# A routed-experts stage: the experts' order made ahead of the early tokens, and the next norm's squares partly summed by DVE

## The chip, the core and the metric

The kernel runs on one core of a Trainium2 chip. The metric is the device time of one execution in microseconds (us). Engines: TensorE (PE: matmuls and transposes, with weight loads PEld that overlap them), VectorE (DVE), ScalarE (ACT), GpSimd (POOL) and SyncE (SP, which issues most DMAs).

## What is computed

Two blocks of a transformer are computed in one program for 512 tokens of 1024 channels, all in 32-bit floats. The first block (a gated delta mixer and a feed-forward) isn't touched. The second has two layers, "even" and "odd"; each is a norm, a mixer, a norm and a layer of experts. The experts are what matters here:

```python
h = _rms(x, norm2_w[layer]) * (1 + scale2) + shift2
x = x + gate2 * _hier_moe(h, ...)

def _hier_moe(h, w_group, b_group, w_expert, b_expert, w1, w3, w2):
    g_logits = xt @ w_group + b_group                 # 4 groups
    g_sel = argmax(g_logits)
    e_logits = (xt @ w_expert + b_expert)             # 8 experts in each group
    top_v, top_i = lax.top_k(e_in, 2)                 # two of the group's eight
    gate = p_g * softmax(top_v)
    # for each of 32 experts e, over its tokens xr:
    (silu(xr @ w1[e]) * (xr @ w3[e])) @ w2[e]         # 1024 -> 512 -> 1024
    # times the gate, summed into the token's row
```

Layer 1 ("odd") begins with a norm of the x that layer 0's experts leave: x / sqrt(mean(x*x) + eps), times a weight.

## The kernel before

x stands transposed in on-chip memory, as 8 pieces (k = 0 to 7) of 128 channels by 512 tokens. `experts(layer, ...)` is one block in which each engine runs a list of steps of its own; the engines meet only through semaphores, and each list is worked off in order. The block runs twice, from about 1690 to 2230 us (layer 0) and from about 2545 to the end (layer 1).

**Routing** (`route`). PE makes the logits (L2556 to L2565), transposes h to rows of tokens, which ACT stores in HBM for the gathers, and counts the tokens of each expert (L2571 to L2578). DVE makes from these, in a long list of small steps, first the selection matrices A of the two experts that are always computed first ("early", `FIXED` = 2), then the `order` of all experts by their count of tokens (L2669 to L2677), then for each token its slot (L2681 to L2737). `do(...)` is an instruction after which DVE waits for itself, since the next one reads its result. PE multiplies A with the rows (L2583) to have expert 0's tokens transposed, and makes the numbers of expert 1's tokens (L2589); DVE copies these (L2673) for POOL's gather of expert 1 (L2884). When DVE's list has come to L2737, PE makes the tokens of each slot (L2596), DVE copies them (L2739) for the other gathers, and PE spreads slots and weights over rows (L2601), which ACT copies out.

**Experts**. There are 15 units (`KINDS = "wwqpwpqwpwqwppq"`): "w" is one expert with a tile of 128 slots, "p" two experts with 64 each, "q" four with 32 each. Each expert has six loads of weights of 1 MB: four for `hidden` (w1 and w3, L2917), two for `output` (w2, L2941). SP issues all loads in order of use (L2823) into a ring of `MOE_RING` = 14 slots: load n waits until PE has used load n - 14. The first ten belong to experts 0 and 1, so they need no order. Ahead of load 10 SP waits for the order (L2841) and reads the numbers of the experts from it.

PE's list for unit i: the first half of `hidden(i)`, `turn(i + 1)` (transposes of the gathered tokens, L2900, which wait for the gather), `aturn(i - 1)` (L2927), the second half of `hidden(i)`, `output(i - 1)`, `scattered(i - 2)` (L2955: eight products that bring the rows back to the tokens, one for each k). In unit 0 the placing (L2596, L2601) stands after the second half of `hidden(0)`. After each of the scattered products DVE adds the result, times the gate, to x (`add`, L3081). Two banks are used for these in turn, so product n waits for add n - 2.

**Tail**. For the last unit the list is: output half 0, scattered k = 0 to 3, output half 1, scattered k = 4 to 7. DVE's list: adds 0 to 3, `out` (the copy of half 1's result, L3067), adds 4 to 7. In layer 0 ACT squares each piece of x when its add is through (`norm_squares`, L2806), and PE sums the squares over the channels with a matrix of ones, one product for each k (`norm_totals`, L2811): those of k = 0 to 3 ahead of output half 1, those of k = 4 to 7 after the last scattered product. ACT makes the norm's factor from the sum (L3049, L3050). A product of 32-bit floats appears as two records in the trace.

Of the kernel before, what the change touches and what calls it, by code (L numbers as in the profile page):

```python
# [17 lines left out]
ALU = mybir.AluOpType  # L18
# [5 lines left out]
KD = D // P  # L24
# [10 lines left out]
FIXED = 2  # L35
# [114 lines left out]
class Program:  # L150
# [1228 lines left out]
    squares = 0  # L1379
# [1113 lines left out]
    def route(self, layer):  # L2493
# [8 lines left out]
        def new(a, b):  # L2502
# [36 lines left out]
        s = {n: self.sem("route_" + n) for n in ["lg", "turned", "kept", "stored", "e", "ex", "oh", "rank", "ab", "tok",  # L2539
                                                 "order", "slots", "early", "early_made", "halves", "halves_kept", "early_tok",  # L2540
                                                 "place_made", "placed"]}
# [6 lines left out]
        toks, early_toks = small[:, 320:320 + BLOCKS], self.bank[4][:, 0:FIXED]  # L2548
# [72 lines left out]
        def vector_steps(dve):  # L2621
            def do(ins):
                self.dve.after(dve, ins)
# [45 lines left out]
            do(dve.tensor_tensor(kf, self.C("bonus"), cn, ALU.add))  # L2669
            do(dve.tensor_tensor(grid, across(key), rows32(key), ALU.is_gt))  # L2670
            do(dve.tensor_reduce(pf, grid, AX.X, ALU.add))
            dve.wait_ge(s["early_made"], 1)
            dve.tensor_copy(self.early_tok[:, 1:FIXED], early_toks[:, 1:FIXED]).then_inc(s["early_tok"], 1)  # L2673
            do(dve.tensor_tensor(grid, across(place), counted, ALU.is_equal))
            do(dve.tensor_tensor(grid, grid, c3("iota_e", 32), ALU.mult))  # L2675
            do(dve.tensor_reduce(picked.rearrange("p a b -> p (a b)"), grid, AX.X, ALU.add))  # L2676
            dve.tensor_copy(self.order, picked.rearrange("p a b -> p (a b)")).then_inc(s["order"], 1)  # L2677

            dve.wait_ge(s["ex"], 2)

# [62 lines left out]
    def experts(self, layer, job, gate):  # L2743
# [22 lines left out]
        N = len(seq)  # L2766
# [4 lines left out]
        for i in range(N - 1):  # L2771
            first13[i] = n
            n += 4 * len(seq[i][1])
            if i >= 1:
# [8 lines left out]
        s = {n: self.sem("moe_" + n) for n in ["turned", "kept0", "kept1", "used", "silu", "a", "aturned", "akept",  # L2783
                                               "yk0", "yk1", "spread", "scatter", "summed", "added"]}
# [8 lines left out]
        def spares(eng):  # L2793
            return eng.value_load(self.spare[0:1, OVF:OVF + 1], min_val=0, max_val=OVF) > 0
# [6 lines left out]
        spare_added = self.sem(f"moe_spare{layer}_added")  # L2801
        if layer == 0:
            sq, ss, squares = self.sem("odd1_squares"), self.sem("odd1_sums"), self.view(f, KD, L)

        def norm_squares(act, k):
            act.activation(squares[:, k, :], self.x[:, k, :], ACT.Square).then_inc(sq, 1)  # L2806

        def norm_totals(pe, ks):
            for k in ks:
                pe.wait_ge(sq, k + 1)  # L2810
                mm = pe.matmul(self.bank[0][:, :], self.C("ones"), squares[:, k, :], start=(k == 0), stop=(k == KD - 1))  # L2811
            if ks[-1] == KD - 1:
                mm.then_inc(ss, 1)

        with nc.Block() as block:
            @block.sync
# [74 lines left out]
            def _(pe):  # L2891
# [86 lines left out]
                aturn(N - 1)  # L2978
                output(N - 1, [0])
                scattered(N - 1, [0])  # L2980
                if layer == 0:
                    norm_totals(pe, range(4))
                output(N - 1, [1])
                scattered(N - 1, [1])
                if layer == 0:
                    norm_totals(pe, range(4, KD))
                with pe.If(any_spare):
                    pe.wait_ge(s["added"], KD * N)
                    spare_tensor(pe)
                    if layer == 0:  # L2990
                        pe.wait_ge(spare_added, KD * OVF)
                        pe.wait_ge(sq, 2 * KD)
                        norm_totals(pe, range(KD))

            @block.scalar
            def _(act):
# [55 lines left out]
            @block.vector  # L3052
            def _(dve):
                def keep(i):
                    dve.wait_ge(s["turned"], i + 1)
                    dve.tensor_copy(xT[i % 2][:, 4:8, :], self.bank[1][:, :].rearrange("p (a b) -> p a b", a=4)  # L3056
                                    ).then_inc(s["kept1"], 1)

                def akeep(i):
                    dve.wait_ge(s["aturned"], i + 1)  # L3060
                    dve.tensor_copy(aT, self.bank[6][:, :].rearrange("p (a b) -> p a b", a=4)).then_inc(s["akept"], 1)

                def out(i):
                    dve.wait_ge(s["used"], end2[i])
                    if i >= 2:
                        dve.wait_ge(s["summed"], KD * (i - 1))
                    dve.tensor_copy(y[i % 2][:, 512:1024], self.bank[6][:, :]).then_inc(s["yk0"], 1)  # L3067

                def spread(i):
                    if i == 0:  # L3070
                        dve.wait_ge(self.placed, 4)
                    if i >= 2:
                        dve.wait_ge(s["summed"], KD * (i - 1))
                    if i >= 1:
                        dve.wait_ge(s["scatter"], i)
                    self.spread(dve, scatter[i % 2], seq[i][0], s["spread"], i + 1).then_inc(s["scatter"], 1)

                def add(i, ks=range(KD)):
                    for k in ks:
                        dve.wait_ge(s["summed"], KD * i + k + 1)  # L3080
                        dve.scalar_tensor_tensor(self.x[:, k, :], self.bank[4 + k % 2][:, :], gate[:, k:k + 1],  # L3081
                                                 self.x[:, k, :], ALU.mult, ALU.add).then_inc(s["added"], 1)

                self.scale_steps(dve, [job], scaled)
                route_vector(dve)
                def gated(i):
                    dve.wait_ge(s["silu"], i + 1)
                    dve.tensor_tensor(a[i % 2], a[i % 2], self.bank[3][:, :], ALU.mult).then_inc(s["a"], 1)  # L3088

                for i in range(N - 1):  # L3090
                    if FIXED <= i + 1 < N:
                        keep(i + 1)
                    if i >= 1:
                        akeep(i - 1)
                    gated(i)
                    if i >= 1:
                        out(i - 1)
                    if i >= 2:
                        add(i - 2)
                    if i >= 1:  # L3100
                        spread(i - 1)
                akeep(N - 2)
                add(N - 3)
                spread(N - 2)
                out(N - 2)
                add(N - 2)
                spread(N - 1)
                any_spare = spares(dve)
                gated(N - 1)
                akeep(N - 1)  # L3110
                add(N - 1, [0, 1, 2, 3])
                out(N - 1)
                add(N - 1, [4, 5, 6, 7])
                if layer == 0:
                    self.gains(dve, self.S("norm1_2", 8, 16), self.mod["odd"][:, 8:16])
                with dve.If(any_spare):
                    dve.wait_ge(s["added"], KD * N)
                    spare_vector(dve)
# [291 lines left out]
```

## Time and profile before

| what | us |
|---|---|
| median of 3 runs (lowest, highest) | 3090.06 (3087.45, 3093.63) |
| profiled execution, its own time | 3087.26 |
| its span in the trace | 3085.5 |
| PE busy | 2816.3 (91%) |
| DVE busy | 1483.2 (48%) |
| ACT busy | 645.0 (21%) |
| DMA queue q1, share of the 16 engines | 48.1% |
| mean granted clock of PE | 0.953 |

The busy shares are means over stages of very different kinds, and a busy PE isn't PE at full speed: its clock is granted at one of two levels, and the column PEclk gives it as a share of the full one. The experts stages are to be read by themselves, with windows, timelines and what ended the idle time of an engine.

### The profile page before, as it was taken

The numbers are of one execution on the slowest core, as the hardware profiler recorded it, in microseconds if no ns is written. First come the engines' busy times: TensorE is split into PE (matmuls) and PEld (weight loads), VectorE is DVE, ScalarE is ACT, GpSimd is POOL, SyncE is SP. The second block draws the span as 40 slices with busy tenths as digits, with TensorE's granted clock in tenths as the row PEclk, the third lists the DMA queues.
The fourth block names the chain that finished last, engine by engine and source line by source line (L and its number), as shares of the span: only waits on it lengthen the run. The fifth ranks groups of instructions, "written<-read, shape, count | busy, mean of one in ns | idle before, by whom it ended". The sixth has DMA issues, their size and how long they took to land. (4 is left out here: it accounts for less than half of the span.)

```text
span 3085.5 us, 36648 instructions
## 1 busy us (share of the span) xinstructions
PE 2816.3 (91%) x14052; PEld 1813.9 (59%) x14052; DVE 1483.2 (48%) x2937; ACT 645.0 (21%) x1350; POOL 158.1 (5%) x169
## 2 busy tenths in 40 slices
PE   6989779999988998999889989999799899899997
PEld 4877657788946887877764533333278545333332
DVE  4576565566735677336543423324355724333334
ACT  3111454445621111010232100000202422000000
POOL 0000021212200000000010000000000000000000
PEclk8999989999999999999979999999999998999999
DMA  6111146663022232222103799999632036999997
GB/s 249 50 46 55 69 152 246 246 246 137 15 95 69 82 90 74 83 69 78 60 1 143 287 420 419 420 419 420 241 112 82 15 153 231 410 418 419 420 419 313
DMA packets 112920, 614.83 MB, mean 199 GB/s; under 512 B 12944, under 2 KB 13408, under 8 KB 62944
## 3 DMA queue, kind: packets, MB, share of 16 engines
q1 hardware_dynamic: 102464, 576.67, 48.1%
q0 software_dynamic: 9120, 31.49, 2.9%
q10 hardware_dynamic: 1152, 4.19, 0.3%
q8 instruction: 118, 1.93, 0.3%
q14 instruction: 66, 0.54, 0.1%
HBM read 603.79 MB, written 8.51 MB: 198 GB/s over the span
## 5 line engine op out<-in xcount | busy, mean ns | idle before, releaser
L2917 PE MATMUL bank<-arena 128*32 128x512 f32 (+2 forms) x2048 | 429.6, 602 | 15.8 <-DMA arena<-in_w 14.8
L440 PE MATMUL bank<-arena 128*128 128x256 f32 x1776 | 411.9, 387 | 33.2 <-DVE arena L493 10.8
L440 PEld LDWEIGHTS bank<-arena 128*128 128x128 f32 x1776 | 341.6, 193 | 99.6 <-issue 34.5
L2917 PEld LDWEIGHTS bank<-arena 128*32 128x32 f32 (+2 forms) x2048 | 148.6, 134 | 269.8 <-issue 268.9
L2941 PE MATMUL bank<-arena 128*32 128x512 f32 (+2 forms) x1024 | 230.8, 661 | 36.4 <-DMA arena<-in_w 36.4
L2955 PE MATMUL bank<-arena 128*128 128x512 f32 x480 | 235.4, 614 | 10.5 <-DVE arena L3129 4.9
L253 PE MATMUL bank<-arena 128*128 128x512 f32 (+1 forms) x608 | 217.4, 517 | 14.8 <-DVE arena L652 13.9
L3081 DVE SCALAR_TENSOR_TENSOR arena<-bank,arena 128x512 f32<-128x512 f32 x240 | 180.3, 751 | 81.3 <-PE bank L2955 68.5
L2941 PEld LDWEIGHTS bank<-arena 128*32 128x32 f32 (+2 forms) x1024 | 78.3, 143 | 184.9 <-issue 184.8
L253 PEld LDWEIGHTS bank<-arena 128*128 128x128 f32 x608 | 119.3, 197 | 110.2 <-issue 101.5
L2955 PEld LDWEIGHTS bank<-arena 128*128 128x128 f32 x480 | 76.6, 188 | 167.2 <-DVE arena L3081 96.5
L3088 DVE TENSOR_TENSOR arena<-arena,bank 128x512 f32<-128x512 f32 x30 | 20.7, 688 | 220.1 <-ACT arena L3023 220.1
L2999 ACT ACTIVATE arena<-bank 128x512 f32<-128x512 f32 x30 | 17.9, 597 | 504.7 <-PE bank L2900 480.2
L3067 DVE COPY arena<-bank 128x512 f32<-128x512 f32 x30 | 20.8, 692 | 205.2 <-PE bank L2941 205.2
L1475 PE MATMUL bank<-arena 128*128 128x256 f32 x528 | 118.0, 379 | 0.0
L1111 ACT ACTIVATE arena<-bank 128x256 f32<-128x256 f32 x288 | 93.6, 382 | 88.3 <-PE bank L1031 65.9
L1475 PEld LDWEIGHTS bank<-arena 128*128 128x128 f32 x528 | 100.0, 189 | 14.4
L1031 PE MATMUL bank<-arena 128*128 128x128 f32 x576 | 98.4, 293 | 1.7 <-DVE arena L1226 1.0
L1031 PEld LDWEIGHTS bank<-arena 128*128 128x128 f32 x576 | 75.3, 190 | 40.0 <-issue 31.6
L1223 DVE TENSOR_TENSOR arena<-bank,arena 128x256 f32<-128x256 f32 x144 | 61.0, 424 | 76.8 <-PE bank L1016 76.7
L1016 PE MATMUL bank<-arena 128*128 128x128 f32 x576 | 94.4, 287 | 0.6
L3056 DVE COPY arena<-bank 128x512 f32<-128x512 f32 x26 | 18.0, 692 | 148.9 <-PE bank L2900 148.9
(452 smaller groups left out, 4152.3 us busy)
## 6 DMA issues: line engine op xcount, KB each, us to landing
arena<-in_w SPq DMA_DIRECT2D x384, 1024.0 KB, 19.4
arena<-in_dense SPq DMA_DIRECT2D x308, 512.0 KB, 4.5
arena<-core_rows POOLq DMA_DIRECT2D x48, 256.0 KB, 6.6
arena<-in_xT SPq DMA_DIRECT2D x2, 2048.0 KB, 12.6
token_rows<-arena ACTq DMA_DIRECT2D x8, 512.0 KB, 2.6
gdn_gate<-arena POOLq DMA_DIRECT2D x8, 256.0 KB, 2.6
arena<-gdn_gate SPq DMA_DIRECT2D x1, 2048.0 KB, 8.3
arena<-band_bias POOLq DMA_DIRECT2D x2, 1024.0 KB, 6.0
```

What stands on the lines that cost most here:

```text
L253: mm = eng.matmul(dst, w[:, k, :], src[:, k, :], start=(k == 0), stop=(k == KD - 1))
L440: mm = pe.matmul(out, w[:, k, :], x[:, k, :], start=(k == 0), stop=(k == K1 - 1))
L1016: mm = pe.matmul(Y[u][:, q, :], buf[u]["bl"][:, q, :], buf[u]["xl"][:, u, q, :], start=True, stop=True)
L1031: mm = pe.matmul(touched(X[u][:, 2 * q:2 * q + 2, :], l, u), buf[u]["zs"][:, q, :], buf[u]["yn"][:, q, :], start=False, stop=(l == 6), ski ...
L1111: act.activation(gathered(buf[u]["xl"][:, side, :, :], l + 1), touched(X[u], l + 1, side), ACT.Copy).then_inc(kept, 1)
L1223: dve.tensor_tensor(buf[u]["yn"], Y[u][:, 0:2, :], levels[:, l - 1, :, :].to_broadcast([P, 2, P]), ALU.mult).then_inc(s["yn"], 1)
L1475: mm = pe.matmul(product(m, p), s4[:, t, k, :], ht[:, t, k, :], start=(k == 0), stop=(k == K1 - 1))
L2917: mm = pe.matmul(self.bank[2 + t][part, :], xT[i % 2][:, 2 * q + k, part], w[j][:, k, t, :], start=(q == 0 and k == 0), stop=(q == 3 and k ...
L2941: mm = pe.matmul(self.bank[7 - t][part, :], aT[:, k, part], w[j][:, k, :], start=(k == 0), stop=(k == 3))
L2955: pe.matmul(self.bank[4 + k % 2][:, :], y[i % 2][:, k * P:(k + 1) * P], scatter[i % 2], start=True, stop=True).then_inc(s["summed"], 1)
L3067: dve.tensor_copy(y[i % 2][:, 512:1024], self.bank[6][:, :]).then_inc(s["yk0"], 1)
L3081: dve.scalar_tensor_tensor(self.x[:, k, :], self.bank[4 + k % 2][:, :], gate[:, k:k + 1], self.x[:, k, :], ALU.mult, ALU.add).then_inc(s[" ...
```

## The change

In three places of `route` and `experts`:

1. `route`, DVE's list: the wait for PE's early tokens and their copy (L2673) move from ahead of L2674 to behind L2677. The order is then made ahead of the copy. This holds in both layers.
2. `experts`, tail of layer 0: PE no longer multiplies each of the eight pieces of squares with the ones. DVE adds the squares of k = 1 to 6 to those of k = 0 in place, three sums behind add 3 and ahead of `out`, one behind add 5, one behind add 6, one behind add 7. Each waits for ACT's square, and all but the last are followed by a wait of DVE for itself. PE multiplies the gathered sum and, apart from it, the squares of k = 7, with the ones (two products), both behind the last scattered product.
3. The rare case in which an expert has more tokens than its slots hold (`any_spare`) calls `norm_totals` over all eight as before.

The scattered products and the output halves keep their places.

```diff
@@ route, DVE
             do(dve.tensor_reduce(pf, grid, AX.X, ALU.add))
-            dve.wait_ge(s["early_made"], 1)
-            dve.tensor_copy(self.early_tok[:, 1:FIXED], early_toks[:, 1:FIXED]).then_inc(s["early_tok"], 1)
             do(dve.tensor_tensor(grid, across(place), counted, ALU.is_equal))
             do(dve.tensor_tensor(grid, grid, c3("iota_e", 32), ALU.mult))
             do(dve.tensor_reduce(picked.rearrange("p a b -> p (a b)"), grid, AX.X, ALU.add))
             dve.tensor_copy(self.order, picked.rearrange("p a b -> p (a b)")).then_inc(s["order"], 1)
+            dve.wait_ge(s["early_made"], 1)
+            dve.tensor_copy(self.early_tok[:, 1:FIXED], early_toks[:, 1:FIXED]).then_inc(s["early_tok"], 1)
@@ experts, PE
                 scattered(N - 1, [0])
-                if layer == 0:
-                    norm_totals(pe, range(4))
                 output(N - 1, [1])
                 scattered(N - 1, [1])
                 if layer == 0:
-                    norm_totals(pe, range(4, KD))
+                    pe.wait_ge(gathered_sums, 1)
+                    pe.matmul(self.bank[0][:, :], self.C("ones"), squares[:, 0, :], start=True, stop=False)
+                    pe.wait_ge(sq, KD)
+                    pe.matmul(self.bank[0][:, :], self.C("ones"), squares[:, KD - 1, :], start=False, stop=True).then_inc(ss, 1)
@@ experts, DVE
+                def sum_square(k):
+                    dve.wait_ge(sq, k + 1)
+                    return dve.tensor_tensor(squares[:, 0, :], squares[:, 0, :], squares[:, k, :], ALU.add)
+
                 add(N - 1, [0, 1, 2, 3])
+                if layer == 0:
+                    for k in range(1, 4):
+                        self.dve.after(dve, sum_square(k))
                 out(N - 1)
-                add(N - 1, [4, 5, 6, 7])
+                add(N - 1, [4, 5])
+                if layer == 0:
+                    self.dve.after(dve, sum_square(4))
+                add(N - 1, [6])
+                if layer == 0:
+                    self.dve.after(dve, sum_square(5))
+                add(N - 1, [7])
+                if layer == 0:
+                    sum_square(6).then_inc(gathered_sums, 1)
                 if layer == 0:
                     self.gains(dve, self.S("norm1_2", 8, 16), self.mod["odd"][:, 8:16])
```

## Rows read from the trace of the kernel before

**Rows 1.** The page, costliest groups: busy and mean ns, then idle time and its releaser.

```profile
L2941 PE MATMUL bank<-arena 128*32 128x512 f32 (+2 forms) x1024 | 230.8, 661 | 36.4 <-DMA arena<-in_w 36.4
```

**Rows 2.** Windows of 10 us: length, PE, PEld, DVE, ACT, POOL busy, PEclk, DMA share, GB/s.

```profile
1750.00:1760.00 10.00, 10.00 (x24) 4.35 (x23) 1.03 (x2) 0.78 (x2) 0.23 (x1) 1.00 0.89 310
1770.00:1780.00 10.00, 9.91 (x83) 3.94 (x80) 1.53 (x3) 1.20 (x2) 0.94 (x1) 1.00 1.01 423
...
2210.00:2220.00 10.00, 9.45 (x46) 3.05 (x44) 3.05 (x5) 2.52 (x4) 0.00 (x0) 1.00 0.01 4
```

**Rows 3.** Timeline of PE, layer 0: start, duration, engine, line, operation, count, idle before.

```profile
1721.54 1.04 PE L2900 MATMUL bank<-arena 128*128 128x128 f32 x8
1722.41 7.05 PE L2917 MATMUL bank<-arena 128*128 128x512 f32 x16
1732.81 3.59 PE L2596 MATMUL bank<-arena 128*128 128x31 f32 x16 [3.35 <-DVE arena L2737]
...
1741.10 7.05 PE L2917 MATMUL bank<-arena 128*128 128x512 f32 x16
```

**Rows 4.** Timeline of DVE, POOL and SP's queue in the routing of layer 0.

```profile
1714.25 0.16 DVE L2673 CAST arena<-bank 128x1 uint32<-128x1 f32 x1 [7.06 <-PE bank L2589]
...
1715.25 1.19 POOL L2884 DMA_INDIRECT arena<-token_rows,arena  x1 [115.26 <-DVE arena L2673]
...
1718.09 0.18 DVE L2677 CAST arena<-arena 128x32 int32<-128x32 f32 x1
1718.18 0.16 DVE L2681 TENSOR_REDUCE arena<-arena 128x4 f32<-128x16 f32 x1
...
1720.91 42.81 SPq L2823 DMA_DIRECT2D arena<-in_w  x14
```

**Rows 5.** Short windows, columns as in rows 2: PE's clock around two gaps.

```profile
1732.00:1733.00 1.00, 0.19 (x1) 0.22 (x2) 0.63 (x3) 0.00 (x0) 0.00 (x0) 0.50 0.98 410
1738.00:1739.00 1.00, 1.00 (x8) 1.00 (x7) 0.00 (x0) 0.60 (x1) 0.82 (x1) 0.60 1.02 426
...
1914.00:1917.00 3.00, 0.51 (x6) 0.21 (x4) 0.69 (x1) 0.60 (x1) 0.00 (x0) 1.00 1.01 421
```

**Rows 6.** POOL's gathers: all 28, then the one issued at 1749.29 (DMA view).

```profile
DMA to landing us min/median/max: 4.5/8.6/9.9
...
arena<-token_rows,arena POOLq DMA_INDIRECT x1, 5.9
```

**Rows 7.** Timeline of layer 1: POOL's gather of expert 1 and PE.

```profile
2572.28 1.25 POOL L2884 DMA_INDIRECT arena<-token_rows,arena  x1 [285.90 <-DVE arena L2673]
2578.62 1.04 PE L2900 MATMUL bank<-arena 128*128 128x128 f32 x8
...
2589.90 3.59 PE L2596 MATMUL bank<-arena 128*128 128x31 f32 x16 [3.36 <-DVE arena L2737]
...
2599.66 7.05 PE L2917 MATMUL bank<-arena 128*128 128x512 f32 x16
```

**Rows 8.** Timeline of the tail of layer 0.

```profile
2181.36 0.69 DVE L3129 TENSOR_TENSOR arena<-arena 128x512 f32<-128x512 f32 x1
...
2211.61 1.61 DVE L3081 SCALAR_TENSOR_TENSOR arena<-bank,arena 128x512 f32<-128x512 f32 x2 [0.36 <-PE bank L2955]
...
2212.26 3.60 PE L2811 MATMUL bank<-arena 128*128 128x512 f32 x8
...
2215.80 3.65 PE L2941 MATMUL bank<-arena 128*32 128x512 f32 x32
...
2219.59 0.69 DVE L3067 COPY arena<-bank 128x512 f32<-128x512 f32 x1 [6.37 <-PE bank L2941]
...
2221.50 1.61 DVE L3081 SCALAR_TENSOR_TENSOR arena<-bank,arena 128x512 f32<-128x512 f32 x2 [1.22 <-PE bank L2955]
...
2224.13 3.61 PE L2811 MATMUL bank<-arena 128*128 128x512 f32 x8
...
2225.12 0.63 ACT L2806 ACTIVATE arena<-arena 128x512 f32<-128x512 f32 x1 [0.23 <-DVE arena L3081]
```

More of the change, by code:

```diff
@@ L2803, in experts, with norm_totals @@
             sq, ss, squares = self.sem("odd1_squares"), self.sem("odd1_sums"), self.view(f, KD, L)
+            gathered_sums = self.sem("odd1_gathered_sums")
         def norm_squares(act, k):
             act.activation(squares[:, k, :], self.x[:, k, :], ACT.Square).then_inc(sq, 1)
-        def norm_totals(pe, ks):
-            for k in ks:
-                pe.wait_ge(sq, k + 1)
+        def norm_totals(pe):
+            for k in range(KD):
                 mm = pe.matmul(self.bank[0][:, :], self.C("ones"), squares[:, k, :], start=(k == 0), stop=(k == KD - 1))
-            if ks[-1] == KD - 1:
-                mm.then_inc(ss, 1)
+            mm.then_inc(ss, 1)
         with nc.Block() as block:
@@ L2992, in _ @@
                         pe.wait_ge(sq, 2 * KD)
-                        norm_totals(pe, range(KD))
+                        norm_totals(pe)
             @block.scalar
```

## The prediction

> **What bounds the kernel now.** I read the page first: one core, a span of 3085.5 us, and the largest waits of TensorE (PE) inside the experts stages are on weight loads, 36.4 us of idle time ahead of L2941 over both layers [rows 1]. Next come windows of 10 us over the experts stage of layer 0, for the DMA column. From 1770 us on the queues move 423 GB/s and the 16 engines are full; that goes on for some 390 us with PE waiting now and then. Between 1750 and 1760, however, they move only 310 GB/s [rows 2]. There the ring of 14 slots is full: SP can issue a load only when PE has used a slot, and in the first two experts, which keep whole tiles of tokens ("w"), PE needs about 3.5 us a slot. So near the start of the stage **PE sets the time of the loads**, and from the first block with four experts ("q") on, the loads set the time of PE. Whatever PE gains ahead of about 1763 us moves the whole stream of loads, and with it the end of the stage; what only the loads gain ahead of that point is lost against the full ring. The same holds in layer 1.
>
> So I then read PE's timeline ahead of that point. PE runs the first half of expert 0, turns the tokens of expert 1 (1721.54), runs the second half (1722.41 to about 1729.46), stands idle for 3.35 us on DVE's L2737, does the placing of the slots (L2596, L2601) from 1732.81, and starts expert 1 at 1741.10 [rows 3]. The idle time is the end of DVE's long chain of routing steps. That chain itself was held up before: DVE waited 7.06 us for PE's early tokens (L2673) and only then made the order [rows 4]. The third view is PE's clock in windows of 1 us: in the gap it fell to half (0.50, that is 1.2 of 2.4 GHz) by 1732 and came back only within 1738 to 1739 [rows 5].
>
> **The order of the experts ahead of the tokens (both layers).** The four instructions L2674 to L2677 move into DVE's wait of 7.06 us. The order, ready at 1718.27 now, is then ready about 7.1 us earlier, at 1711.2. The copy of the early tokens waits for PE as before and stays at 1714.25, so the gather that POOL issues at 1715.25 isn't issued later. What stands behind the copy (L2681 on) starts at 1714.4 in place of 1718.18, 3.8 us earlier [rows 4], and the chain's end, now 1732.8, comes at 1729.0: just ahead of PE, which is through with expert 0 at 1729.46 [rows 3]. The idle time of 3.35 us closes; next late is PE itself.
>
> SP issued its first load that depends on the order 2.6 us after the order, at 1720.91 [rows 4]. It will do so at about 1713.8. Four slots are free, and the next ones wait for PE as before. The earlier loads gain nothing by themselves: the load after the first eight has to wait for the first quarter of expert 1 (now 1741.10 + 3.5 = 1744.6), and eight loads of 1 MB at 420 GB/s are through 20 us after their start, before it in either kernel.
>
> But they take something. Today the gather of expert 1's tokens (0.5 MB, issued at 1715.25) runs on idle DMA engines: it lands after 4.5 us, the minimum of all 28 gathers [rows 6], at 1719.75, and PE wants it at 1721.54 [rows 3]. In the changed kernel 4 MB of weights are ahead of it in the engines, 10 us of work. Beside a full queue 24 of the 28 gathers landed after 8.0 to 9.9 us, median 8.6; beside a queue with one load or so it was 5.9 [rows 6]. Here the queue is full, so I take 8.6: landing at 1723.85, and **PE waits 2.3 us at the turn of expert 1**, which delays its second half and all behind it. Bounds: 0 (5.9 and below) and 3.6 us (9.9). Layer 1 has the same: issue 2572.28, wanted at 2578.62, so 8.6 gives 2.3 us [rows 7].
>
> The trace shows both kinds of DMA, SP's loads and POOL's gather, slowing each other down [rows 6]. The Trainium skill, "DMA: Bandwidth & Descriptors", section "Issuing engines are not separate DMA queues", says the same in general: copies issued by different engines end up on the same 16 DMA engines and interleave. Its section "Queues, rings and completion order" adds that an engine takes turns between the queues, which would leave the gather a half share and speaks for the rival "gather in time" below; the trace's 8.6 beside 4.5 speaks against it.
>
> **The clock while slots are placed.** L2596 and L2601 are 48 records of small matmuls. At half clock they took 8.29 us in layer 0 (1732.81 to 1741.10) [rows 3], partly, as the clock came back in their midst, and 9.76 us in layer 1 [rows 7]. At full clock eight records of the kind take 0.87 us (1721.54 to 1722.41) [rows 3], 0.109 each, so 48 take 5.2 us. Without the gap the clock has no reason to fall there: I book 3.1 us for layer 0 and 4.5 us for layer 1. Bounds: nothing, if it falls all the same, and these values.
>
> The new wait of 2.3 us is a gap of its own. In the 3 us from 1914, of which PE worked 0.51, a gap of 2.49, the clock stayed at 1.00 [rows 5], and the gap in which it fell was 3.35 us [rows 3]. I take it that it stays, but not by much. If it falls there, it is at half for 6.8 us as from 1732 to 1738.7 [rows 5], and costs 3.4 us in that layer.
>
> Layer 0: 3.35 - 2.3 + 3.1 = 4.1 us gained; layer 1: 3.36 - 2.3 + 4.5 = 5.6 us [rows 3, 7].
>
> **The sums of squares by DVE (layer 0 only).** Two groups of eight records (four products each) with the ones matrix, 3.54 and 3.61 us, leave PE [rows 8]. The first stood ahead of the last output half (2212.26, output at 2215.80), on the chain, and its 3.54 us are gained: the queues move 4 GB/s from 2210 on [rows 2], so the weights have landed, and DVE isn't late for the copy L3067 (2219.59, then 2216.05): its adds 0 to 3 end at 2213.22, and three sums at some 0.73 us (0.69 of L3129 and its own wait) end at 2215.4 [rows 8]. They are covered by 0.6 us; without it they would cost their own length less that. L391 and L392 come later by the same time as the last sum and are wanted by nobody before the norm is made. The scatters stay where they stand, so none is added or moved.
>
> The second group is replaced by three more sums on DVE's chain and two products (four records). Taken from the first late add (2221.50 now): adds 4 and 5 end at +1.61, sum 4 at +2.34, add 6 at +3.13, sum 5 at +3.85, add 7 at +4.63, sum 6 at +5.35; ACT's last square, begun at the end of add 7 (+3.62 now), ends at +5.29. PE starts at +5.45 and needs 4 x 0.43 and the last drain, 1.9 us: +7.35. Now its eight records run from 2224.13 (+2.63) to +6.24 [rows 8]. So 1.1 us is given back: net 2.4 us. PE is idle for about 2.9 us ahead of them, and if the clock falls there, four records take 1.7 us more; net 0.7 us. The next stage starts when all engines are out of this one, so the gain is carried on.
>
> **Sum.** 4.1 + 5.6 + 2.4 = 12.1 us. The profiled execution took 3087.26 us (span 3085.5), 2.8 below the median of the runs; I subtract from the median: 3090.06 - 12.1 = 3078.0 us.
>
> **The rivals.**
> "Clock falls at the new wait": for it speaks that 2.3 us is near gaps at which it fell, against it the gap of 2.49 us. One layer: 12.1 - 3.4 = 8.7, 3081.4 us; both: 5.3, 3084.8 us.
> "Gather in time": it lands in under 6.3 us as if the queue were nearly empty, because each engine serves it in turn. PE doesn't wait: 12.1 + 4.6 = 16.7, 3073.4 us. For it speaks the 5.9 us gather; against it 24 of 28.
> "The placing stays at half clock", because the tiny matmuls don't keep it: 1.0 + 1.1 + 2.4 = 4.5 us, 3085.6 us. Against it: the clock in the rows fell in the idle stretch, not in the matmuls.
> "Gather behind the backlog" (the other side): the engines work off SP's six loads first, 6 MB or 15 us from 1714.9 (1.1 after the first issue, an estimate), then the gather, which lands at about 1732; PE waits 10.6 us a layer and its clock falls: layer 0 is 3.35 - 10.6 + 3.1 - 3.4 = 7.5 us worse, layer 1 6.2, less 2.4 of the tail: 11.3 us slower, 3101.4 us. It decides the sign from the point at which the wait passes 5 us (12.1 - 6.8 = 2 x 2.65 beyond the 2.3 booked), a landing of some 11.3 us, which none of the 28 had.
> That the order doesn't come earlier at all can't be: nothing else holds the four instructions.
>
> **How the numbers follow.** Forecast 0.40; the clock falls at the wait in one layer 0.25, in both 0.09; gather in time 0.10; placing at half clock 0.10; gather behind the backlog 0.06. The runs before spread by 6 us, and a measurement can tell about 0.2%, 6 us. Faster by more: forecast, one layer and gather in time, 0.75, less 0.07 because 8.7 us is near the border: 0.68. Within: 0.26, slower 0.06. The range goes from just under the gather in time to just over the placing at half clock, 3071.5 to 3087, which leaves out the backlog and the edges.
>
> **What would show it.** Right: L2677 ahead of L2673 at about 7 us before where it stood; SP's first load near 1713.8; an idle time of some 2.3 us of PE ahead of the L2900 of expert 1 with the gather as its releaser; none ahead of L2596; clock 1.00 through L2596 and L2601, and about 5.2 us for both; L2941's last half right behind the scatters; four records of the ones matrix that start about 5.4 us after add 4. Wrong: a gather that lands in 5 us, clock 0.50 at the turn of expert 1 or in the placing, or an end of the stage that doesn't move with the start of expert 1.

## The result and the profile after

The changed kernel takes 3081.96 us (median of 8 runs, 3077.2 to 3084.16), the kernel before, run on the same chips, 3092.64 us (8 runs, 3087.45 to 3098.32). The ratio is 0.9964 [0.9953, 0.9975]: **11.1 us faster**, 7.7 to 14.5. The forecast was 3078.0 us (3071.5 to 3087.0), a gain of 12.1 us. Time, range and sign held. The reasons held less well than the total, as the traces show. The profiled execution took 3077.2 us, 10.1 less than the one of before.

The page of the changed kernel: the span, and the group that answers to [rows 1] (L2940 is before's L2941, `output`).

```profile
span 3074.4 us, 36633 instructions
...
L2940 PE MATMUL bank<-arena 128*32 128x512 f32 (+2 forms) x1024 | 232.2, 664 | 36.4 <-DMA arena<-in_w 36.4
```

PE's waits on the weights of `output` are the same 36.4 us; with those of `hidden` the page has 49.0 us in all, where before it was 51.2. They hardly shrink, although experts start earlier: the stream of loads from HBM still bounds the middle of the stage. What changed stands at its two ends.

**Start of the stage, layer 0.** Timeline of the changed kernel, to be held against [rows 3, 4]: start, duration, engine, line, operation, count, idle time before it and its releaser. L2916 is `hidden`, L2899 `turn`, L2883 the gather, L2822 SP's loads; L2675 now makes the order, L2677 copies the early tokens.

```profile
1706.83 0.18 DVE L2675 CAST arena<-arena 128x32 int32<-128x32 f32 x1
1709.60 0.16 DVE L2677 CAST arena<-bank 128x1 uint32<-128x1 f32 x1 [2.60 <-PE bank L2589]
1709.64 47.71 SPq L2822 DMA_DIRECT2D arena<-in_w  x14
1710.00 7.12 PE L2916 MATMUL bank<-arena 128*128 128x512 f32 x16 [0.43 <-issue]
1710.61 1.03 POOL L2883 DMA_INDIRECT arena<-token_rows,arena  x1 [114.14 <-DVE arena L2677]
1719.88 1.76 PE L2899 MATMUL bank<-arena 128*128 128x128 f32 x8 [2.76 <-DMA arena<-token_rows,arena]
1721.44 8.10 PE L2916 MATMUL bank<-arena 128*128 128x512 f32 x16
1729.37 1.86 PE L2596 MATMUL bank<-arena 128*128 128x31 f32 x16
1731.08 3.82 PE L2601 MATMUL bank<-arena 128*128 128x128 f32 x32
1734.73 7.05 PE L2916 MATMUL bank<-arena 128*128 128x512 f32 x16
```

Read it from above. The order is there 2.8 us ahead of the early tokens' copy, where it used to come 4 us behind, and DVE's wait for PE has shrunk from 7.06 to 2.60 us. SP starts its loads 0.4 us before PE starts expert 0; before, 6.3 us after. POOL's gather is issued 1 us behind them, among them. PE then stands idle 2.76 us at the turn of expert 1, with the gather as releaser: a wait that the kernel before doesn't have. There is no gap ahead of the placing (L2596) any more, and the placing takes 5.36 us (1729.37 to 1734.73) in place of 8.29.

How long the first transfers took (DMA view of the changed kernel; the last number is us from issue to landing):

```profile
arena<-in_w SPq DMA_DIRECT2D x2, 1024.0 KB, 8.8
arena<-token_rows,arena POOLq DMA_INDIRECT x1, 9.2
```

The gather of 0.5 MB, which took 4.5 us on idle DMA engines, takes 9.2, in both layers.

PE's clock in windows of 1 us, columns as in [rows 2], the clock behind POOL's share:

```profile
1719.00:1720.00 1.00, 0.12 (x1) 0.12 (x2) 0.86 (x6) 0.00 (x0) 0.00 (x0) 1.00 0.97 406
1720.00:1721.00 1.00, 1.00 (x6) 1.00 (x7) 0.90 (x4) 0.00 (x0) 0.00 (x0) 0.57 1.03 434
1722.00:1723.00 1.00, 1.00 (x2) 0.34 (x1) 0.97 (x2) 0.98 (x3) 0.00 (x0) 0.50 0.97 410
1723.00:1724.00 1.00, 1.00 (x3) 0.53 (x2) 0.96 (x3) 1.00 (x1) 0.00 (x0) 0.72 1.03 434
1730.00:1731.00 1.00, 1.00 (x12) 1.00 (x11) 0.00 (x0) 0.17 (x1) 0.00 (x0) 1.00 0.99 246
```

The clock fell behind the new wait, from about 1720.1, and was back within 1723 to 1724; in the placing it stands at 1.00. From the start of the turn to that of the placing it is 9.49 us (1719.88 to 1729.37); where the same work ran at full clock, in e3_loads_after_gather below, it is 7.75 (1724.68 to 1732.43). The dip costs 1.7 us.

Layer 1 shows the same (timeline of the changed kernel, against [rows 7]):

```profile
2563.11 7.12 PE L2916 MATMUL bank<-arena 128*128 128x512 f32 x16 [0.43 <-issue]
2572.95 1.51 PE L2899 MATMUL bank<-arena 128*128 128x128 f32 x8 [2.72 <-DMA arena<-token_rows,arena]
2574.26 8.36 PE L2916 MATMUL bank<-arena 128*128 128x512 f32 x16
2582.45 1.86 PE L2596 MATMUL bank<-arena 128*128 128x31 f32 x16
2587.81 7.05 PE L2916 MATMUL bank<-arena 128*128 128x512 f32 x16
```

**Tail of layer 0.** Timeline of the changed kernel, against [rows 8]: L3113 are DVE's sums, L2984 and L2986 the two products with the ones, L3049 ACT's factor of the norm.

```profile
2201.39 1.61 DVE L3081 SCALAR_TENSOR_TENSOR arena<-bank,arena 128x512 f32<-128x512 f32 x2 [12.73 <-PE bank L2954]
2204.11 3.65 PE L2940 MATMUL bank<-arena 128*32 128x512 f32 x32
2204.88 2.14 DVE L3113 TENSOR_TENSOR arena<-arena 128x512 f32<-128x512 f32 x3
2207.96 0.69 DVE L3067 COPY arena<-bank 128x512 f32<-128x512 f32 x1 [0.94 <-PE bank L2940]
2209.87 1.61 DVE L3081 SCALAR_TENSOR_TENSOR arena<-bank,arena 128x512 f32<-128x512 f32 x2 [1.22 <-PE bank L2954]
2214.16 0.68 DVE L3113 TENSOR_TENSOR arena<-arena 128x512 f32<-128x512 f32 x1
2214.90 1.94 PE L2984 MATMUL bank<-arena 128*128 128x512 f32 x2 [2.24 <-DVE arena L3113]
2216.63 1.91 PE L2986 MATMUL bank<-arena 128*128 128x512 f32 x2
2218.58 0.69 ACT L3049 ACTIVATE arena<-bank,arena 128x512 f32<-128x512 f32 x1 [2.37 <-PE bank L2986]
```

Two rows of the kernel before that are needed beside [rows 8], its add 0 and its factor:

```profile
2209.64 1.61 DVE L3081 SCALAR_TENSOR_TENSOR arena<-bank,arena 128x512 f32<-128x512 f32 x2 [12.84 <-PE bank L2955]
...
2227.77 0.69 ACT L3049 ACTIVATE arena<-bank,arena 128x512 f32<-128x512 f32 x1 [0.72 <-PE bank L2811]
```

The three early sums are hidden: DVE still waits 0.94 us for PE before it copies (L3067). From add 0 (2201.39) to add 4 (2209.87) it is 8.48 us; before it was 11.86 (2209.64 to 2221.50). That is the booked gain, 3.4 for 3.54. From add 4 to the factor, however, it is 8.71 us (2209.87 to 2218.58), where before it was 6.27 (2221.50 to 2227.77): 2.4 us given back in place of 1.1. PE was idle for 2.24 us ahead of L2984, and the clock was half behind it (window of the changed kernel):

```profile
2215.00:2216.00 1.00, 1.00 (x2) 0.49 (x3) 0.13 (x1) 1.00 (x1) 0.00 (x0) 0.54 0.00 0
```

**What the pair of traces adds up to.** From expert 0's start to expert 1's start: 26.52 and 28.00 us before (layer 0, layer 1), 24.73 and 24.70 after, so 1.8 and 3.3 us gained. The tail, from add 0 to the first step behind the norm, went from 19.93 to 18.84 us: 1.1. Together 6.2 us, while the spans differ by 11.1. Of that, 4.6 us lie ahead of expert 0, which begins at 1714.58 in the one trace and at 1710.00 in the other. DVE, too, reaches the moved place some 4 us earlier (at 1703.05, three instructions of 3.7 us ahead of 1706.83, against 1707.2, where its wait of 7.06 us began), so all but some 0.4 us of the difference is older than the first edited instruction. In the other traces of this study expert 0 begins anywhere from 1711.0 to 1717.7, whatever the edit; with one part of the change alone it begins at 1715.87 (e1) and 1713.79 (e2), so neither part brings the early start with it. Two spans alone would have made the gain look larger than what the edits did at their places.

### The profile page after: what moved, and what is told of

It is laid out like the page before. It is cut to its first block and busy times, and to the rows that moved or that the text cites. A ratio compares the mean times of both kernels' runs of the same rounds, so it can differ in the third digit from the quotient of the medians.

```text
span 3074.4 us, 36633 instructions
## 1 busy us (share of the span) xinstructions
PE 2808.3 (91%) x14040; PEld 1806.5 (59%) x14040; DVE 1486.5 (48%) x2943; ACT 645.5 (21%) x1350; POOL 158.0 (5%) x169
## 5 line engine op out<-in xcount | busy, mean ns | idle before, releaser
L2916 PE MATMUL bank<-arena 128*32 128x512 f32 (+2 forms) x2048 | 430.3, 600 | 13.5 <-DMA arena<-in_w 12.6
L440 PE MATMUL bank<-arena 128*128 128x256 f32 x1776 | 410.9, 386 | 33.4 <-DVE arena L493 10.9
L440 PEld LDWEIGHTS bank<-arena 128*128 128x128 f32 x1776 | 340.6, 193 | 100.9 <-issue 34.6
L2916 PEld LDWEIGHTS bank<-arena 128*32 128x32 f32 (+2 forms) x2048 | 149.5, 134 | 267.5 <-issue 266.5
L2940 PE MATMUL bank<-arena 128*32 128x512 f32 (+2 forms) x1024 | 232.2, 664 | 36.4 <-DMA arena<-in_w 36.4
L2940 PEld LDWEIGHTS bank<-arena 128*32 128x32 f32 (+2 forms) x1024 | 78.9, 143 | 185.6 <-issue 185.0
L3088 DVE TENSOR_TENSOR arena<-arena,bank 128x512 f32<-128x512 f32 x30 | 20.7, 688 | 216.2 <-ACT arena L3023 216.2
L3067 DVE COPY arena<-bank 128x512 f32<-128x512 f32 x30 | 20.8, 692 | 201.8 <-PE bank L2940 201.8
```

Source lines behind the costliest of these rows:

```text
L440: mm = pe.matmul(out, w[:, k, :], x[:, k, :], start=(k == 0), stop=(k == K1 - 1))
L2916: mm = pe.matmul(self.bank[2 + t][part, :], xT[i % 2][:, 2 * q + k, part], w[j][:, k, t, :], start=(q == 0 and k == 0), stop=(q == 3 and k ...
L2940: mm = pe.matmul(self.bank[7 - t][part, :], aT[:, k, part], w[j][:, k, :], start=(k == 0), stop=(k == 3))
```

## The experiments

All ran beside the kernel before. "Start" is the time from expert 0's start to expert 1's, "stream" the time from expert 0's start to that of the last unit's first output half (the last work that waits for weights), each for layer 0 / layer 1, in us.

| kernel | time, us (runs) | against before, us (interval) | start | stream |
|---|---|---|---|---|
| before | 3092.64 (8) | | 26.5 / 28.0 | 487.1 / 489.5 |
| after | 3081.96 (8) | -11.1 (-14.5 to -7.7) | 24.7 / 24.7 | 483.6 / 487.4 |
| e1_order_only | 3085.67 (11) | -5.9 (-9.0 to -2.8) | 24.9 / 25.0 | 487.4 / 486.3 |
| e2_squares_only | 3089.65 (11) | -1.2 (-4.0 to +1.5) | 27.9 / 28.0 | 489.5 / 489.7 |
| e3_loads_after_gather | 3075.36 (5) | -17.0 (-21.6 to -12.7) | 20.1 / 20.1 | 484.4 / 483.8 |
| e4_sum_early | 3078.42 (5) | -12.4 (-16.4 to -8.0) | 24.9 / 24.8 | 487.9 / 489.5 |
| e5_hold_and_tail | 3074.44 (4) | -16.4 (-20.7 to -12.1) | 20.1 / 20.1 | 483.6 / 484.0 |
| e6_loads_later | 3096.11 (1) | one run | 20.1 / 20.1 | 493.9 / 494.1 |
| e7_best | 3073.49 (6) | -16.7 (-21.0 to -12.4) | 20.1 / 20.1 | 483.3 / 483.5 |
| e8_pe_kept_busy | 3081.57 (1) | one run | 24.7 / 24.8 | 487.3 / 487.5 |

### Each part alone

`e1_order_only` is the kernel before with the order's move alone:

```diff
-            dve.wait_ge(s["early_made"], 1)
-            dve.tensor_copy(self.early_tok[:, 1:FIXED], ...).then_inc(s["early_tok"], 1)
             do(dve.tensor_tensor(grid, across(place), counted, ALU.is_equal))
...
             dve.tensor_copy(self.order, ...).then_inc(s["order"], 1)
+            dve.wait_ge(s["early_made"], 1)
+            dve.tensor_copy(self.early_tok[:, 1:FIXED], ...).then_inc(s["early_tok"], 1)
```

> The kernel before with the first part alone: order ahead of the early tokens, squares as before. My theory (the gain comes from PE's closed gap ahead of the placing and the clock kept there, less PE's new wait for the gather): from expert 0's first record to expert 1's about 24.7 us in both layers, as in the changed kernel, against 26.5 and 28.0 before; so 1.8 + 3.3 us in the two places, 5 us or, with what the stream of loads makes of it, up to 9 us faster than before. Rival (the part is worth nothing since loads that start earlier run into a wait anyway): within 2 us of before, and all of the gain in the other run, the squares.

`e2_squares_only` is the changed kernel with this move undone, so that only the tail of layer 0 differs from before:

> The kernel before with the second part alone: DVE sums the squares, order as before. My theory: 3.5 us gained at the output half, 1.1 us given back at the end with PE at full clock, 2.8 at half clock: 0.7 to 2.4 us faster than before, with the last ones products starting 5.0 to 5.5 us after add 4. Rival (the end of the stage is set by DVE's chain and the whole gain is given back): 0 or slower. The changed kernel was 11 us faster, of which its trace shows 4.6 us as arisen ahead of the first edited instruction: if the placement of code and not chance made those, one of the two single parts shows them too.

Measured: the order alone gives 5.9 us, the squares alone 1.2 us that can't be told from nothing. In e1 the wait at the turn is 2.95 and 3.02 us, the gather lands after 9.4 us, and the placing takes 5.36 us: all three belong to the order's move. In e2 add 4 to the factor takes 8.24 us, and the tail 18.37 us against 19.93: 1.6 us by its trace. What follows: the order carries the change. The two parts add up to 7.1 us, less than the 11.1 of both together, but the intervals overlap.

### The new wait belongs to the loads ahead of the gather

`e3_loads_after_gather` keeps the early order, but SP waits until the gather of expert 1 has landed before it issues loads that depend on the order:

```diff
                         sp.wait_ge(self.order_ready, 1)
+                        sp.wait_ge(x_in[1], x_in_before[1] + nth(1))
```

> The changed kernel, with SP waiting for the landing of expert 1's gather ahead of its first load that depends on the order. My theory (PE's wait of 2.8 us at the turn of expert 1 is the gather slowed by loads that nobody needs so early, and the ring has room): the gather lands after some 4.5 us in place of 9.2, PE's wait at L2899 goes, its clock stays full, expert 0 to expert 1 takes 20.5 us in place of 24.7, and the time falls by 2 x 4.3 = 8 to 9 us against the changed kernel, 20 us against before. Rival (the loads are needed early: the stream starts 6 us later and PE waits for weights instead): no gain or a loss against the changed kernel, with more DMA waits on the first q unit near 1765.

Measured: 3075.36 us, 17.0 less than before and 6.6 less than the changed kernel's median. The gather lands after 4.3 us. PE doesn't wait at the turn, which takes 1.03 us without idle time before it, and the start falls to 20.07 us in both layers. SP's first load now goes out 7.6 us after expert 0's start, later than in the kernel before (6.3), and it costs two waits on weights, 1.3 and 0.4 us, in the stretch from 1700 to 1800. So the wait of 2.8 us and the dip of the clock behind it come from the order's effect on the loads, and nothing of the order's gain comes from loads that start early.

`e6_loads_later` holds the loads still longer, until PE has used four slots:

```diff
                         sp.wait_ge(x_in[1], x_in_before[1] + nth(1))
+                        sp.wait_ge(s["used"], 4)
```

> The kernel with SP held until the gather landed, and held further until PE has used four slots, which is 14.8 us after expert 0's start: first load at about 17.5 us in place of 7.6. My theory (the loads have slack of a few us only: four free slots and four that PE frees early, 20 us of work, have to be through when PE frees the next at 23.6 us, and in the six frees after it the stream catches up 6 us): expert 0 to expert 1 stays 20.1 us, but PE's first waits for weights come in the first q unit near 42 to 60 us after expert 0's start, together 6 to 10 us in each layer, and the time is 10 to 20 us above the run with SP held. Rival (the start of the stream doesn't matter since the ring is full anyway): the same time as with SP held.

Measured (one run): 3096.11 us, some 21 more than e3, where 10 to 20 were expected. Experts 0 and 1 run as in e3. The first load comes 17.6 us after expert 0's start, and then the stream is late (e6_loads_later: SP's queue, PE, and its waits from 1700 to 1800):

```profile
1729.83 30.11 SPq L2822 DMA_DIRECT2D arena<-in_w  x18
...
1767.87 6.45 PE L2918 MATMUL bank<-arena 128*32 128x512 f32 x32 [4.97 <-DMA arena<-in_w]
...
1778.94 6.04 PE L2918 MATMUL bank<-arena 128*32 128x512 f32 x32 [4.63 <-DMA arena<-in_w]
...
PE bank L2918 <- DMA arena<-in_w: 9.6, 2, 5.0
```

Two waits of 5 us appear in the first block of four experts, and the stream ends 10 us a layer later than in e3. The prediction's picture of the stage is shown by this pair: loads that begin 7.6 us after expert 0's start cost PE next to nothing, loads that begin at 17.6 us set the time of the whole stream.

### The tail

In `e4_sum_early` DVE adds only k = 1 to 3. PE multiplies their sum ahead of the last scattered products, and then k = 4 to 7 one by one as in the kernel before:

```diff
@@ PE
                 output(N - 1, [1])
-                scattered(N - 1, [1])
                 if layer == 0:
                     pe.wait_ge(gathered_sums, 1)
                     pe.matmul(self.bank[0][:, :], self.C("ones"), squares[:, 0, :], start=True, stop=False)
-                    pe.wait_ge(sq, KD)
-                    pe.matmul(self.bank[0][:, :], self.C("ones"), squares[:, KD - 1, :], start=False, stop=True).then_inc(ss, 1)
+                scattered(N - 1, [1])
+                if layer == 0:
+                    for k in range(4, KD):
+                        pe.wait_ge(sq, k + 1)
+                        mm = pe.matmul(self.bank[0][:, :], self.C("ones"), squares[:, k, :], start=False, stop=(k == KD - 1))
+                    mm.then_inc(ss, 1)
@@ DVE
                 out(N - 1)
-                add(N - 1, [4, 5])
...
+                add(N - 1, [4, 5, 6, 7])
```

> The changed kernel with another tail: DVE sums the squares of k = 0 to 3 only, PE multiplies that sum in its gap ahead of the last scattered products, and multiplies k = 4 to 7 one by one behind them, as before. My theory (the second group's sums on DVE cost 2.4 us at the end: DVE's chain is longer and PE's clock falls while it waits): from add 4 to the norm's factor 6.3 us in place of 8.7, so 2 to 3 us faster than the changed kernel. Rival (the end is bound by ACT's squares, or the product in the gap holds up the scattered ones): no difference within 1 us, scattered products starting 0.9 us later.

Measured: 3078.42 us, 12.4 less than before. Its tail (e4_sum_early, timeline; L3084 is add 4):

```profile
2215.28 1.12 PE L2983 MATMUL bank<-arena 128*128 128x512 f32 x2
...
2217.41 1.61 DVE L3084 SCALAR_TENSOR_TENSOR arena<-bank,arena 128x512 f32<-128x512 f32 x2 [1.22 <-PE bank L2954]
...
2220.04 3.60 PE L2988 MATMUL bank<-arena 128*128 128x512 f32 x8
2223.68 0.69 ACT L3052 ACTIVATE arena<-bank,arena 128x512 f32<-128x512 f32 x1 [0.72 <-PE bank L2988]
```

Add 4 to the factor takes 6.27 us again, and the whole tail 16.73 us in place of 18.84 (after) and 19.93 (before). So by the traces the sum of the early squares is worth 3.2 us, and adding the late ones on DVE gave 2.1 of them back. Between the times of e4 and of the changed kernel (12.4 and 11.1 us gained) such a step can't be made out; where it went is shown under "Both together".

`e8_pe_kept_busy` asks why the late ones cost so much. It is the changed kernel with two products of squares with the ones that nobody uses, put into PE's gap:

```diff
                 if layer == 0:
+                    pe.wait_ge(sq, 4)
+                    for k in (1, 2):
+                        pe.matmul(self.bank[1][:, :], self.C("ones"), squares[:, k, :], start=(k == 1), stop=(k == 2))
                     pe.wait_ge(gathered_sums, 1)
```

> The changed kernel with two more products (four records, results unused) on PE behind the last scattered product, ahead of its wait for the gathered sum. My theory (the four records of the sum took 3.7 us since PE's clock fell in its gap of 2.2 us; DVE's chain is the other part of what was given back): with PE busy through the gap the clock stays 1.00, the four records take 1.9 us, and from add 4 to the norm's factor it is 7.0 us in place of 8.7. Rival (the records are slow for another reason, or the clock falls all the same): 8.7 us as before.

Measured (one run; e8_pe_kept_busy, timeline and a window of its tail; L2985 are the added products, L2987 and L2989 those of the sums):

```profile
2215.41 1.61 DVE L3084 SCALAR_TENSOR_TENSOR arena<-bank,arena 128x512 f32<-128x512 f32 x2 [1.22 <-PE bank L2954]
...
2218.04 1.88 PE L2985 MATMUL bank<-arena 128*128 128x512 f32 x4
...
2220.45 1.12 PE L2987 MATMUL bank<-arena 128*128 128x512 f32 x2 [0.53 <-DVE arena L3116]
2221.41 1.02 PE L2989 MATMUL bank<-arena 128*128 128x512 f32 x2
2222.47 0.69 ACT L3052 ACTIVATE arena<-bank,arena 128x512 f32<-128x512 f32 x1 [0.71 <-PE bank L2989]
...
2221.00:2222.00 1.00, 1.00 (x4) 0.36 (x2) 0.00 (x0) 0.76 (x1) 0.00 (x0) 1.00 0.09 25
```

With PE's gap down to 0.53 us the clock stands at 1.00, and add 4 to the factor takes 7.06 us. Against the 8.71 of the changed kernel that is 1.65 us: the clock. The other 0.8 us (7.06 against 6.27) is DVE's chain of sums itself. Work that nobody uses made the step shorter, which excludes that DVE's chain alone was the cause.

### Both together

`e5_hold_and_tail` is e3 with the tail of e4. `e7_best` has the same tail, with the hold put at the first load that depends on the order, in `load(n)`:

```diff
+                    if n == first13[FIXED]:
+                        sp.wait_ge(x_in[1], x_in_before[1] + nth(1))
                     if n >= MOE_RING:
```

> The same with SP held ahead of its reading of the experts' numbers, as in the run with SP held. My theory: its gain (17 us) and the tail's (2 to 3 us) add up: 19 us faster than before. Rival (they don't add, since what the tail gives goes into a wait for the next stage's weights): 17 us.

> The order ahead of the tokens, the gather of expert 1 protected, and the tail in which DVE sums only the squares of k = 0 to 3. SP waits for the gather at its first load that depends on the order, behind its reading of the experts' numbers (in the run before it waited ahead of the reading). My theory (in the run with SP held, PE's way from expert 0 to expert 1 was 20.1 us, 7.9 less than before, of which 4.9 a layer were left at the stage's end; the tail gave 3.2 us): 20.1 us again, SP's first load some 5 us after expert 0's start in place of 7.6, and 2 x 5 + 3 = 13 to 19 us faster than before, about 3073 us. Rival (the loads ahead of PE's need it were late by the holding, and a hold 2.6 us shorter gives back what was lost): 5 us or more faster than the run with SP held and the late sums.

Measured: 3074.44 and 3073.49 us, 16.4 and 16.7 less than before. Start of layer 0 in e7_best, a timeline and then the gather in the DMA view (L2901 is `turn`, L2824 SP's loads):

```profile
1711.03 7.12 PE L2918 MATMUL bank<-arena 128*128 128x512 f32 x16 [0.43 <-issue]
1716.10 3.09 SPq L2824 DMA_DIRECT2D arena<-in_w  x6
1717.99 1.03 PE L2901 MATMUL bank<-arena 128*128 128x128 f32 x8
...
arena<-token_rows,arena POOLq DMA_INDIRECT x1, 4.3
```

The first load goes out 2.5 us earlier than in e3 (5.07 against 7.56 us after expert 0's start) with no gain that can be seen: the slack of the loads once more. Nor does the tail of e4 show on top of the hold: 16.4 and 16.7 against 17.0, each within some 4 us, while the tails in the traces promise some 2. The traces show where it went, and it isn't a wait for the next stage's weights: from the tail's end (the first step behind the norm) to the next stage's first product (L440) it is 7.4 to 7.6 us with either tail. It went into PE's clock behind that. Of L440's records, the second group in the changed kernel and in e5 (timelines):

```profile
2236.55 1.97 PE L440 MATMUL bank<-arena 128*128 128x256 f32 x8 [2.91 <-DVE arena L493]
...
2237.11 2.84 PE L440 MATMUL bank<-arena 128*128 128x256 f32 x8 [3.64 <-DVE arena L493]
```

In all three kernels with the tail of e4 the first group ran at full clock from its start (5.13 us in e5, where it is 5.86 in the changed kernel), PE's gap behind it is 3.64 us in place of 2.91, and behind the gap the clock fell to half, which it didn't in the changed kernel. From L440's first record to the first one of a later step, L1801, it is 22.7 us in e4, e5 and e7, and 21.1 in the changed kernel, e3 and e6; and on to layer 1's expert 0 it is 337.3 to 337.5 against 335.3 to 335.4. That takes back the 2 us. Whether it must isn't shown, since kernels with one and the same tail differ there too: before and e1 (334.8 and 337.5), the changed kernel and e2 (335.3 and 336.5).

e3, e5 and e7 can't be told apart. All three beat the changed kernel's median, by 6.6 to 8.5 us. Their intervals against before overlap with that of the changed kernel, but only two of their 15 runs took longer than its fastest of eight, and in the traces expert 1 starts 4.6 us sooner after expert 0 in both layers.

## Why the prediction was right, and where it wasn't

**What bounds the kernel: right, but not all of a gain is carried.** The first two experts are PE's, the rest the loads': e3, e6 and e7 show both ends of it. The prediction then passed every microsecond gained at expert 1's start on to the end of the stage. Over all traces the start was 27.6 us (before and e2), 24.8 (after, e1, e4) and 20.1 (held: e3, e5, e7), and the stream's end 489.0, 487.1 (with e8's) and 483.8. Of 2.8 us gained 1.9 arrive, and of 7.5 us 5.2: **about two thirds**. The second pair is the firm one (the six held streams lie within 483.3 to 484.4, the four of before and e2 within 487.1 to 489.7); the single streams of the first scatter from 483.6 to 489.5, more than the 1.9 us themselves. A part of the loss are longer waits for weights, 51.2 us on the page of before, 53.9 in e3 and 52.1 in e7. Another shows at the wait about 327 us behind expert 0's start of layer 0: in the changed kernel PE goes on at 326.2, in before at 328.4, in e7 at 321.6. Behind it the same 32 products took 5.13 us in before and 6.61 in e7, as the clock was half behind the wait for more or less of them. That is up to 1.5 us; the rest isn't settled.

**DVE's order: right.** Ahead of the early tokens by 2.8 us, SP's first load 0.4 us before expert 0's start (forecast: 0.8 before), the gather issued no later (0.6 us behind expert 0's start, where it was 0.7), the gap of 3.35 us ahead of the placing gone in both layers. In both layers the placing came behind expert 0 without a wait.

**The gather: right in kind and nearly in size.** 9.2 us to land for 8.6, a wait of 2.76 and 2.72 for 2.3. The median of the gathers beside a full queue was the right row to take; "gather in time" and "gather behind the backlog" fell. The wait cost 0.4 us a layer more than booked. That SP's loads and the gather slow *each other* down is not in [rows 6], which shows the gather's side alone.

**The placing's clock: right.** 5.36 us for 5.2, at 1.00. "The placing stays at half clock" fell: the small matmuls keep the clock if PE comes to them without a gap.

**The clock at the new wait: the step that failed.** "I take it that it stays" rested on the one gap of 2.49 us in [rows 5]. It fell in both layers, which was the rival with 0.09, and in all six further waits of this kind (e1, e4, e8). Its price, though, was half of what the rival said: half speed for about 3.4 us, not the 6.8 of [rows 5], so 1.7 us a layer, not 3.4. With this, the sum at expert 1's start is, for layer 0, 3.35 - 2.76 + 2.93 - 1.74 = 1.8 us (measured 1.8, booked 4.1), and for layer 1 3.36 - 2.72 + 4.40 - 1.75 = 3.3 us (measured 3.3, booked 5.6). The terms close, so no other effect is missing there.

One gap at full clock was no ground for the step, and the traces show it with a gap that has the same length and the same work ahead of it in every kernel. PE multiplies 16 records of a unit's scatter, four records of `aturn`, waits 2.45 us for DVE and goes on with the next scatter. In layer 1 of before, then of the changed kernel (timelines):

```profile
3015.84 7.96 PE L2955 MATMUL bank<-arena 128*128 128x512 f32 x16 [2.45 <-DVE arena L3129]
...
3004.00 9.35 PE L2954 MATMUL bank<-arena 128*128 128x512 f32 x16 [2.46 <-DVE arena L3144]
```

The first runs at full clock, the second has half of it for 3.4 us and takes 1.4 us more. Over the ten traces and two layers this wait left the clock alone 8 times (7.96 us) and lowered it 12 times (9.35 to 9.57 us).

**The tail: the gain right, what was given back too small.** The early group's 3.54 us came off as booked and the three sums were hidden, with 0.94 us to spare for the 0.6 forecast. In the late part PE waited 2.24 us for the 2.9 forecast, the clock fell, and 2.4 us in place of 1.1 were given back. The prediction had named this end (net 0.7) and not taken it; measured is 1.1 in the pair of traces, 1.6 in e2. Both misses are one: a short gap of PE was taken to leave the clock alone, three times, and three times it didn't. In the tail the clock fell in all four kernels that have the gap of 2.24 us (the changed kernel, e2, e3, e6).

**The total: right in part because two errors met.** By the prediction's own steps, mended with the traces, the change is worth 6.2 us at its places, and less if only two thirds of the starts are carried (3.4 + 1.1 = 4.5 us). The two parts run alone add up to 7.1 us. The interval of the changed kernel, 7.7 to 14.5, lies above the traces' sums of 6.2 and 4.5. Part of the distance may be the kernel before, whose median was 3092.64 us in the eight runs beside the changed kernel, 3091.47 in the 21 beside e1 to e4 and 3089.77 in the 11 beside e5 and e7; against 3091.47 the changed kernel would be 9.5 us faster, against 3089.77 7.8. By these medians 2 to 5 us stay without a cause that a trace shows, and this is left open. The forecast of 12.1 overestimated the edits by some 6 us, and the remainder filled most of that: that the total came within 1 us of the forecast is luck.

## What to carry to other kernels

Before a load is made to start earlier, look at what is small, urgent and issued beside it: here 4 MB of weights that had 7 us of slack and more doubled the time of a 0.5 MB gather that had under 2 us (it landed at 1719.75 and was wanted at 1721.54), and one wait of the issuing queue for that gather gave about 6 us more than the change itself. A gap of 2 to 3 us in TensorE's work is to be booked with a dip of the clock behind it (some 1.7 us here), even where a trace shows that very gap at full clock: the next trace may not. And if a stage is bound by its loads, pass on only a part of what its first experts gain.

## What the runs showed of the hardware

- PE's clock fell to half behind gaps of 2.72, 2.76 and 2.24 us, though it had stood at 1.00 through one of 2.49 us [rows 5] and, in the changed kernel, through one of 3.52 us (ahead of 1807.00). Neither the length of the gap nor the work ahead of it decides: one and the same gap of 2.45 us lowered the clock 12 times of 20. What does decide, no run varied.
- How long it stays half differs too: 6.8 us behind a gap of 3.35 us [rows 5], about 3.4 us behind one of 2.76. Two unused products in the gap kept it at 1.00 and saved 1.65 us (e8).
- A gather of 0.5 MB by POOL took 4.3 us on idle DMA engines (layer 0 of e3 and e7), and 9.2 to 9.5 us with loads of 1 MB issued about 1 us ahead of it (after, e1). The two such loads issued first took 8.8 us beside it.
- Expert 0 of layer 0 began anywhere from 1710.0 to 1717.7 us, in ten traces, though no edit stands on its path. Single traces are to be compared by segments, not by spans.
